# A contraction-outer first pair, and new places in SBUF, in a transformer layer with split fp32 matmuls

## Chip, cores and metric

One NeuronCore of one Trainium2 chip runs the whole kernel in one launch. The metric is the device time in microseconds. Three runs of the kernel before gave 1034.02, 1034.82 and 1034.90; the median is 1034.82.

## What is computed

One layer of a streaming encoder on 512 tokens of width 1024, all in float32. The reference, cut to what matters:

```python
x = x + 0.5 * swiglu(rms_norm(x, ffn1_norm), ffn1_gate, ffn1_up, ffn1_down)
x = x + hybrid_mixer(rms_norm(x, mix_norm), w_in, ...)      # GLA | diff attention | short conv, then w_out
x = x + 0.5 * swiglu(rms_norm(x, ffn2_norm), ffn2_gate, ffn2_up, ffn2_down)
return rms_norm(x, final_norm)

def swiglu(h, w_gate, w_up, w_down):                        # w_gate, w_up: 1024 x 2816, w_down: 2816 x 1024
    return (jax.nn.silu(h @ w_gate) * (h @ w_up)) @ w_down
```

## The kernel before

Activations stand transposed: features on the 128 partitions, the 512 tokens in the free dimension. x is KT = 8 tiles of 128x512. TensorE works in a float32 format (fp32r) that holds less than float32, so both operands of each large product are split into a high and a low part, and each 128x128x512 block takes three matmuls (`three`, L379 to L383): hi by hi, hi by lo, lo by hi, summed in one PSUM bank.

The operands are made on the chip. ACT makes xg_hi = gain * x (`operand_hi`, L776) and DVE makes xg_lo = gain * x - xg_hi (`operand_lo`, L1061). Weights arrive from HBM in slabs of 128x1024 (up, 8 k-tiles) or 128x1408 (down, 11 k-tiles of the inner 22) in `raw`, a buffer of two slots; slab s lies in slot s % 2. ACT copies a slab to w_hi (`split_hi`, L766), DVE subtracts to get w_lo (`split_lo`, L1052). SP loads slab s when slab s-2 has been split (`lo_ready`), ACT splits it when the product of slab s-2 is through (`slab_used`). Slabs are counted through the kernel: 44 up slabs of FFN 1 (gate and up in turn), 16 down slabs, the mixer's, 8 of w_out, 44, 16.

The division by the root mean square comes after the product, as a factor per token: squares of x are summed over the tiles in sq_sum, TensorE sums them over the partitions (`mean_squares`, L398), ACT takes the root, DVE inverts it into a diagonal (`invert`, L1077), TensorE spreads that over the partitions (`spread_rms`, L406), ACT copies it to rinv. DVE then multiplies the PSUM results of gate and up by rinv (L1109, L1113), ACT applies silu, DVE multiplies the two, and the result is split into h_hi and h_lo, the moving operands of the down products. The mixer leaves its result in mixed_hi and mixed_lo, the moving operands of w_out. Three projections of the mixer are made the other way round, in natural layout: there xg is the stationary operand and w_hi and w_lo move, 384 columns at a time.

At the start SP issues, in this order, the load of slab 0, the eight x tiles, slab 1 and seven small constants. ACT issues the gain's DMA and loads its table for the root. ACT's order of work is then xg_hi of tile 0, split of slab 0, xg_hi of tiles 1 to 7, split of slab 1, the squares of x tiles 4 to 7; DVE's is the low parts in the same order. GpSimd squares x tiles 0 to 3 and adds all eight into sq_sum. TensorE runs WARM_UP = 14 small matmuls on ones, then the product of slab 0 (waiting for each xg_lo in turn), of slab 1, the mean squares, slab 2, the spread, slab 3, and the start products (a table of the attention's bias, and lambda), and from there in loops a pair of slabs for each of the 22 tiles of the inner width.

Every engine's order is written out by hand, and the waits are on counting semaphores. SBUF places follow from the order of the `sb(...)` declarations: each tensor lies behind the one declared before, and what is declared in an inner `with` block is given back at its end, so that the next declarations take the same place. Two lines set the first products:

```python
pe.wait_ge(xg_lo_ready, first_use + k + 1)                  # L418, before each k-tile of the first product
last = product(g + 1, 2 + b, None, n)                       # L440, the up product, after the gate product
```

## Times and profile before

| | |
|---|---|
| median of 3 runs | 1034.82 us (1034.02 to 1034.90) |
| profiled execution: its own time / its span | 1036.32 us / 1034.5 us |
| granted TensorE clock, mean over the span | 0.987 |
| busy: TensorE / DVE / ACT / GpSimd | 98% / 49% / 34% / 9% |
| HBM traffic | 94 MB, 91 GB/s over the span |

Busy shares are averages over the whole span. A TensorE that is busy is not at its peak, since matmuls overlap: what one costs in a dense stretch is read from the distance between the starts of consecutive ones and not from their durations. The profiled execution took 1.5 us more than the median of the runs.

### The profile page before, as it was taken

The page shows a single profiled execution, that of the slowest core. Times are in us where ns is not written, and L with a number is a line of the kernel's source. Part 1 is how long each engine was busy: PE and PEld are TensorE (multiplying, and loading weights), DVE is VectorE, ACT ScalarE, POOL GpSimd, SP SyncE. Part 2 cuts the span into 40 slices and gives each one's busy share as a digit, 9 for nine tenths or more (in the row PEclk, how much of TensorE's full clock was granted, in tenths as well). Part 3 has the DMA queues.
Part 4 walks back from the last instruction along what each step waited for, and adds up shares of the span by engine and source line. Part 5 has one row for each costly group of instructions (what it writes and reads, how often), then busy time and mean ns, then how long its engine had stood idle before and what let it go on. Part 6 is the DMA issues. An engine that isn't in the chain of part 4 may idle for free.

```text
span 1034.5 us, 13356 instructions
## 1 busy us (share of the span) xinstructions
PE 1010.6 (98%) x5044; PEld 832.2 (80%) x5044; DVE 504.9 (49%) x719; ACT 353.8 (34%) x475; POOL 90.2 (9%) x87
## 2 busy tenths in 40 slices
PE   7999999999999999999989999999999999999996
PEld 4888888888888888777878788788888888888886
DVE  7444444444334433767556864444444444423223
ACT  4443434443221222444723233332332232322221
POOL 6000000000012224000012004300000000000002
PEclk8999999999999999999989999999999999999998
DMA  5233223233322225212211113223222222322312
GB/s 177 90 102 100 85 99 101 83 103 113 111 85 95 101 61 163 72 62 67 71 37 62 54 69 102 82 102 101 84 99 101 101 86 96 131 85 88 108 56 82
DMA packets 27457, 94.89 MB, mean 92 GB/s; under 512 B 3760, under 2 KB 5968, under 8 KB 27424
## 3 DMA queue, kind: packets, MB, share of 16 engines
q1 hardware_dynamic: 26384, 92.03, 26.6%
q0 software_dynamic: 896, 2.39, 0.8%
q8 instruction: 22, 0.36, 0.1%
q14 instruction: 11, 0.09, 0.0%
q10 hardware_dynamic: 144, 0.02, 0.0%
HBM read 92.00 MB, written 2.42 MB: 91 GB/s over the span
## 4 chain that ended last, share of the span: by engine, by line
PE 45%; DVE 3%; ACT 1%; issue 1%; POOL 0%; DVEq 0%; POOLq 0%
PE ps L381 14%; PE ps L382 14%; PE ps L383 14%; PE ps L609 1%; DVE x L1190 1%; DVE e_dec L1287 1%; DVE a_comp L1307 0%; ACT w_hi L774 0%; PE ps L641 0%; PE ps L649 0%; PE ps L579 0%; DVE w_lo L1058 0%; DVE states L1333 0%; PE ps L485 0%; DVE e_dec L1314 0%
## 5 line engine op out<-in xcount | busy, mean ns | idle before, releaser
L381 PE MATMUL ps<-xg_hi,w_hi 128*128 128x512 f32 x848 | 336.5, 397 | 7.5 <-DVE w_lo L1058 3.4
L382 PE MATMUL ps<-xg_lo,w_hi 128*128 128x512 f32 x848 | 331.7, 391 | 0.0
L383 PE MATMUL ps<-xg_hi,w_lo 128*128 128x512 f32 x848 | 331.5, 391 | 0.0
L774 ACT ACTIVATE w_hi<-raw 128x1024 fp32r<-128x1024 f32 (+2 forms) x155 | 174.6, 1127 | 456.3 <-PE ps L383 455.3
L1058 DVE TENSOR_TENSOR w_lo<-raw,w_hi 128x1024 fp32r<-128x1024 f32 (+2 forms) x155 | 208.2, 1343 | 191.3 <-ACT w_hi L774 191.2
L381 PEld LDWEIGHTS ps<-xg_hi,w_hi 128*128 128x128 f32 x848 | 160.0, 189 | 52.5 <-issue 8.7
L383 PEld LDWEIGHTS ps<-xg_hi,w_lo 128*128 128x128 f32 x848 | 160.2, 189 | 34.0
L382 PEld LDWEIGHTS ps<-xg_lo,w_hi 128*128 128x128 f32 x848 | 160.3, 189 | 31.8
L381 PE MATMUL ps<-h_hi,w_hi 128*128 128x512 f32 (+1 forms) x374 | 142.9, 382 | 0.0
L383 PE MATMUL ps<-h_hi,w_lo 128*128 128x512 f32 (+1 forms) x374 | 142.7, 382 | 0.0
L382 PE MATMUL ps<-h_lo,w_hi 128*128 128x512 f32 (+1 forms) x374 | 142.7, 382 | 0.0
L1113 DVE TENSOR_TENSOR up_s<-ps,rinv 128x512 f32<-128x512 f32 x44 | 30.4, 691 | 112.7 <-PE ps L383 112.7
L382 PEld LDWEIGHTS ps<-h_lo,w_hi 128*128 128x128 f32 x374 | 70.2, 188 | 15.1
L381 PEld LDWEIGHTS ps<-h_hi,w_hi 128*128 128x128 f32 x374 | 70.2, 188 | 15.1
L383 PEld LDWEIGHTS ps<-h_hi,w_lo 128*128 128x128 f32 x374 | 70.2, 188 | 15.0
L842 ACT ACTIVATE h_hi<-up_s 128x512 f32 (+1 forms) x44 | 27.8, 632 | 85.4 <-DVE up_s L1118 85.4
L1135 DVE SCALAR_TENSOR_TENSOR x<-ps,x 128x512 f32 (+1 forms) x23 | 15.8, 688 | 70.9 <-PE ps L383 70.9
L1109 DVE TENSOR_TENSOR gate_s<-ps,rinv 128x512 f32<-128x512 f32 x44 | 30.4, 691 | 41.0 <-PE ps L383 36.4
L1120 DVE TENSOR_TENSOR h_lo<-up_s,h_hi 128x512 f32 (+1 forms) x44 | 30.4, 692 | 38.8 <-ACT h_hi L842 38.8
L1064 DVE SCALAR_TENSOR_TENSOR xg_lo<-x,gain,xg_hi 128x512 fp32r<-128x512 f32 (+1 forms) x24 | 32.5, 1373 | 13.3 <-ACT xg_hi L778 13.3
L371 POOL TENSOR_TENSOR x<-x,rinv 128x256 f32<-128x256 f32 x6 | 5.4, 926 | 363.2 <-ACT rinv L802 363.2
L381 PE MATMUL ps<-w_hi,xg_hi 128*128 128x384 f32 x96 | 33.2, 346 | 0.0
(171 smaller groups left out, 816.8 us busy)
## 6 DMA issues: line engine op xcount, KB each, us to landing
raw<-up_w SPq DMA_DIRECT2D x88, 512.0 KB, 3.2
raw<-down_w SPq DMA_DIRECT2D x32, 704.0 KB, 4.0
raw<-t_w SPq DMA_DIRECT2D x18, 512.0 KB, 3.3
raw<-out_w SPq DMA_DIRECT2D x8, 512.0 KB, 3.3
raw<-nat_w SPq DMA_DIRECT2D x6, 576.0 KB, 3.9
x<-xT SPq DMA_DIRECT2D x8, 256.0 KB, 5.2
out<-x SPq DMA_DIRECT2D x8, 256.0 KB, 2.3
raw<-nat_w SPq DMA_DIRECT2D x3, 384.0 KB, 3.2
```

Source lines behind the costliest of these rows:

```text
L381: pe.matmul(out_ap, a[0], b[0], start=first, stop=False)
L382: pe.matmul(out_ap, a[0], b[1], start=False, stop=False)
L383: return pe.matmul(out_ap, a[1], b[0], start=False, stop=last)
L609: last = pe.matmul(ps[c * CHUNK:(c + 1) * CHUNK, bank + hd, col + b * CHUNK:col + (b + 1) * CHUNK], a, bb, start=True, stop=True)
L774: act.activation(w_hi[:, slot(s), 0:w], raw[:, slot(s), 0:w], ACT.Copy).then_inc(hi_ready, 1)
L842: act.activation(h_hi[:, m, :], up_s[:, b, :], ACT.Copy).then_inc(h_hi_ready, 1)
L1058: dve.tensor_tensor(w_lo[:, slot(s), 0:w], raw[:, slot(s), 0:w], w_hi[:, slot(s), 0:w], ALU.subtract).then_inc(lo_ready, 1)
L1064: dve.scalar_tensor_tensor(xg_lo[:, k, :], x[:, k, :], gain[:, gi, bass.ds(k, 1)], xg_hi[:, k, :], ALU.mult, ALU.subtract).then_inc(xg_lo_ ...
L1109: dve.tensor_tensor(gate_s[:, b, :], ps[:, b, :], rinv[:], ALU.mult).then_inc(gate_scaled, 1)
L1113: dve.tensor_tensor(up_s[:, b, :], ps[:, 2 + b, :], rinv[:], ALU.mult).then_inc(up_scaled, 1)
L1120: dve.tensor_tensor(h_lo[:, m, :], up_s[:, b, :], h_hi[:, m, :], ALU.subtract)\
L1135: dve.scalar_tensor_tensor(x[:, k, :], ps[:, bank, :], scale, x[:, k, :], ALU.mult, ALU.add)\
```

## The change

It has two parts.

**The first pair.** Slabs 0 and 1 (gate and up of the first inner tile) are no longer two products one after the other. `first_pair` runs over the eight k-tiles on the outside, and inside over the two slabs: six matmuls per k-tile, into banks 0 and 2. The two slabs come in PIECES = 4 pieces of 256 columns (two k-tiles), by eight DMAs on ACT's queue; slab 0 has buffers of its own (first_raw, first_hi, first_lo), slab 1 has slot 1, and slab 2 finds slot 0 free. ACT and DVE split the pieces between the operand tiles. The squares of x are now all ACT's, in eight buffers, and their sum is DVE's; GpSimd has none at the start. The mean squares come after slab 2 (before: after slab 1), the spread in the middle of slab 3 (before: after slab 2). WARM_UP is 24.

**The places.** x, raw, rinv, sq_sum, ones, ident and the small constants are declared last. xg, w_hi and w_lo come first, then h or mixed. In KB per partition, counted from the first of the kernel's tensors, by the declared sizes:

| | before | after |
|---|---|---|
| xg_hi, xg_lo | 16 to 48 | 0 to 32 |
| w_hi, w_lo | 59 to 81 | 32 to 54 |
| h_hi | 87.6 to 131.6 | 54 to 98 |
| h_lo | 131.6 to 175.6 | 98 to 142 |
| mixed_hi, mixed_lo | 87.6 to 119.6 | 54 to 86 |
| x | 0 to 16 | 173.1 to 189.1 |
| raw | 48 to 59 | 189.1 to 200.1 |

The diff, cut to its core:

```diff
-WARM_UP = 14
+WARM_UP = 24
+PIECES = 4
+PIECEW = UPW // PIECES
...
-        x = sb("x", [P, KT, S])
         xg_hi = sb("xg_hi", [P, KT, S], F32R)
         xg_lo = sb("xg_lo", [P, KT, S], F32R)
-        raw = sb("raw", [P, 2, SLOTW])
         w_hi = sb("w_hi", [P, 2, SLOTW], F32R)
         w_lo = sb("w_lo", [P, 2, SLOTW], F32R)
-        rinv = sb("rinv", [P, S])
-        sq_sum = sb("sq_sum", [P, S])
-        ones = sb("ones", [P, P])
...
             sq = sb("sq", [P, S], stack=st)
+            first_raw = sb("first_raw", [P, UPW], stack=st)
+            first_hi = sb("first_hi", [P, UPW], F32R, stack=st)
+            first_lo = sb("first_lo", [P, UPW], F32R, stack=st)
...
-        onehot_s = pT[0:32].rearrange("b a s -> b (a s)")[:, 0:5 * P]
+        onehot_s = dv[0:32].rearrange("b a f -> b (a f)")[:, 5 * P:10 * P]
...
+        sb("end_of_stages", [P, 64])
+        x = sb("x", [P, KT, S])
+        raw = sb("raw", [P, 2, SLOTW])
+        rinv = sb("rinv", [P, S])
...
-            load(0, up_w[0, 0, 0])
             for k in range(KT):
                 sp.dma_start(x[:, k, :], xT[k]).then_inc(x_loaded[k], 16)
-            load(1, up_w[0, 0, 1])
+            load(2, up_w[0, 1, 0])
...
+            load(3, up_w[0, 1, 1])
...
+            def first_pair():
+
+                for k in range(KT):
+                    q, rest = divmod(k, KT // PIECES)
+                    if rest == 0:
+                        if q < PIECES - 1:
+                            pe.wait_ge(piece_lo, 2 * (q + 1))
+                        else:
+                            wait_slab(1)
+                    pe.wait_ge(xg_lo_ready, k + 1)
+                    for s, (_, hi, lo) in enumerate(first_slabs):
+                        kk = slice(k * P, (k + 1) * P)
+                        last = three(ps[:, 2 * s, :], (hi[:, kk], lo[:, kk]), (xg_hi[:, k, :], xg_lo[:, k, :]),
+                                     k == 0, k == KT - 1)
+                        if k == KT - 1:
+                            last.then_inc(slab_used, 1)
...
-                    if isinstance(i, int) and m == 1 and phase == 0:
-                        spread_rms(phase)
-                    if first and phase:
+                    second = isinstance(i, int) and m == 1 and phase == 0
+                    if second or (first and phase):
                         mean_squares(phase)
-                    last = product(g + 1, 2 + b, None, n)
+                    last = product(g + 1, 2 + b, None, n, spread_at=KT // 2 if second else None)
...
             act.dma_start(gain[:], gains).then_inc(gain_loaded, 16)
+            for q in range(PIECES):
+                for s, (first, _, _) in enumerate(first_slabs):
+                    act.dma_start(first[:, piece(q)], up_w[0, 0, s][:, piece(q)]).then_inc(piece_loaded[q], 16)
...
-            for k in range(KT - 4, KT):
-                act.activation(start_sq[k - (KT - 4)], x[:, k, :], ACT.Square).then_inc(start_squared, 1)
+            split_hi(2)
+            for k in range(KT):
+                if k == KT - 1:
+                    act.wait_ge(lo_ready, 1)
+                act.activation(start_sq[k], x[:, k, :], ACT.Square).then_inc(start_squared if k else sq_added, 1)
...
+            split_lo(2)
+            for k in range(1, KT):
+                dve.wait_ge(start_squared, k)
+                dve.wait_ge(sq_added, k)
+                dve.tensor_tensor(sq_sum[:], sq_sum[:], start_sq[k], ALU.add).then_inc(sq_added, 1)
```

How the order of the instructions moves, at three places. (L numbers of the change are those of its own file.) First ACT at the start, up to its third operand tile, before and now:

```order
L764 DMA gain<-gains 128x32
L806 ACT_TABLE_LOAD
L806 ACTIVATE root_scrap<-eps_t 128x1 [waits consts_set]
L778 ACTIVATE xg_hi<-x,gain 128x512 [waits x_loaded0,gain_loaded]
L774 ACTIVATE w_hi<-raw 128x1024 [waits raw_loaded0]
L778 ACTIVATE xg_hi<-x,gain 128x512 [waits x_loaded1]
L778 ACTIVATE xg_hi<-x,gain 128x512 [waits x_loaded2]
```

```order
L793 DMA first_raw<-up_w 128x256
L793 DMA raw<-up_w 128x256
L835 ACT_TABLE_LOAD
L835 ACTIVATE root_scrap<-eps_t 128x1 [waits consts_set]
L807 ACTIVATE xg_hi<-x,gain 128x512 [waits x_loaded0,gain_loaded]
L929 ACTIVATE first_hi<-first_raw 128x256 [waits piece_loaded0]
L929 ACTIVATE w_hi<-raw 128x256
L807 ACTIVATE xg_hi<-x,gain 128x512 [waits x_loaded1]
L807 ACTIVATE xg_hi<-x,gain 128x512 [waits x_loaded2]
```

The first two rows of the second piece are the last of the eight new DMAs, which stand between the gain's DMA and the table load. The hi parts come in quarters.

Second DVE, from slab 1's low half (before) or slab 2's (now) to the diagonal:

```order
L1058 TENSOR_TENSOR w_lo<-raw,w_hi 128x1024 [waits hi_ready]
L1199 TENSOR_TENSOR lamprod<-lamin 48x2 [waits start_loaded]
L1058 TENSOR_TENSOR w_lo<-raw,w_hi 128x1024 [waits hi_ready] x2
L1080 RECIPROCAL rnat<-rnat 128x4 [waits rms_ready]
L1082 TENSOR_SCALAR rinv<-ident,rnat 128x128 [waits dve_result]
```

```order
L1094 TENSOR_TENSOR w_lo<-raw,w_hi 128x1024 [waits hi_ready]
L1245 TENSOR_TENSOR sq_sum<-sq_sum,gate_s 128x512 [waits sq_added,start_squared] x2
L1245 TENSOR_TENSOR sq_sum<-sq_sum,up_s 128x512 [waits sq_added,start_squared] x2
L1245 TENSOR_TENSOR sq_sum<-sq_sum,sq 128x512 [waits sq_added,start_squared]
L1245 TENSOR_TENSOR sq_sum<-sq_sum,rinv 128x512 [waits sq_added,start_squared]
L1245 TENSOR_TENSOR sq_sum<-sq_sum,first_raw 128x512 [waits sq_added,start_squared]
L1247 TENSOR_TENSOR lamprod<-lamin 48x2 [waits start_loaded]
L1094 TENSOR_TENSOR w_lo<-raw,w_hi 128x1024 [waits hi_ready]
L1116 RECIPROCAL rnat<-rnat 128x4 [waits rms_ready]
L1118 TENSOR_SCALAR rinv<-ident,rnat 128x128 [waits dve_result]
```

Seven adds have come to DVE, between the low halves of slabs 2 and 3.

Third TensorE, the last k-tile of the first pair now and the first matmul of slab 2:

```order
L386 MATMUL ps<-xg_hi,first_hi 128x512 [waits xg_lo_ready]
L387 MATMUL ps<-xg_lo,first_hi 128x512
L388 MATMUL ps<-xg_hi,first_lo 128x512
L386 MATMUL ps<-xg_hi,w_hi 128x512
L387 MATMUL ps<-xg_lo,w_hi 128x512
L388 MATMUL ps<-xg_hi,w_lo 128x512
L386 MATMUL ps<-xg_hi,w_hi 128x512 [waits lo_ready]
```

A wait for xg_lo stands before each group of six matmuls, where it stood before each group of three.

## Rows read from the trace of the kernel before

**Rows 1.** The page: busy us (share of the span) and instructions of each engine

```profile
PE 1010.6 (98%) x5044; PEld 832.2 (80%) x5044; DVE 504.9 (49%) x719; ACT 353.8 (34%) x475; POOL 90.2 (9%) x87
```

**Rows 2.** Timeline, TensorE, 0 to 44 us: start, us, instruction, idle before

```profile
1.01 5.32 PE L519 MATMUL ps<-ones 128*128 128x128 f32 x28 [1.01 <-POOL one_t L333]
8.46 0.80 PE L381 MATMUL ps<-xg_hi,w_hi 128*128 128x512 f32 x1 [2.13 <-DVE w_lo L1058]
...
22.02 0.71 PE L381 MATMUL ps<-xg_hi,w_hi 128*128 128x512 f32 x1 [1.26 <-DVE w_lo L1058]
...
29.19 0.95 PE L402 MATMUL ps<-ones,sq_sum 128*128 128x1 f32 x8
30.00 0.49 PE L381 MATMUL ps<-xg_hi,w_hi 128*128 128x512 f32 x1
...
35.58 1.05 PE L410 MATMUL ps<-rinv,ones 128*128 128x128 f32 x8
...
42.02 1.34 PE L392 MATMUL ps<-pT,relb 32*128 32x512 f32 x4
...
43.60 0.50 PE L381 MATMUL ps<-xg_hi,w_hi 128*128 128x512 f32 x1
```

**Rows 3.** Stretches, TensorE: us, busy (instructions), granted clock, DMA share, GB/s

```profile
12.00:19.00 7.00, 4.49 (x15) 1.00 0.16 59
...
22.00:26.00 4.00, 3.98 (x10) 0.57 0.58 168
```

**Rows 4.** Timeline, DVE, 8 to 43 us

```profile
8.32 11.42 DVE L1064 SCALAR_TENSOR_TENSOR xg_lo<-x,gain,xg_hi 128x512 fp32r<-128x512 f32 x7
...
41.84 1.22 DVE L1058 TENSOR_TENSOR w_lo<-raw,w_hi 128x1024 fp32r<-128x1024 f32 x1
```

**Rows 5.** Line L1064, xg_lo: shortest, median and longest duration in ns

```profile
L1064 DVE SCALAR_TENSOR_TENSOR xg_lo<-x,gain,xg_hi x24: 740/1644/1785, 5.6 to 660.3; 128x512 fp32r<-128x512 f32 x16, - x8
```

**Rows 6.** Timeline, TensorE, an up product: two starts 24 matmuls apart

```profile
200.36 0.39 PE L382 MATMUL ps<-xg_lo,w_hi 128*128 128x512 f32 x1
...
205.80 0.39 PE L382 MATMUL ps<-xg_lo,w_hi 128*128 128x512 f32 x1
```

**Rows 7.** Timeline, TensorE, down products: two starts 66 matmuls apart

```profile
300.06 0.40 PE L382 MATMUL ps<-h_lo,w_hi 128*128 128x512 f32 x1
...
315.46 0.40 PE L382 MATMUL ps<-h_lo,w_hi 128*128 128x512 f32 x1
```

**Rows 8.** Timeline, TensorE, natural layout: two starts 27 matmuls apart

```profile
385.75 0.33 PE L382 MATMUL ps<-w_lo,xg_hi 128*128 128x384 f32 x1
...
390.43 0.33 PE L382 MATMUL ps<-w_lo,xg_hi 128*128 128x384 f32 x1
```

**Rows 9.** Groups by form, TensorE: count, busy us, mean ns of one

```profile
L382 PE MATMUL ps<-xg_lo,w_hi 128*128 128x512 f32 x848 | 331.7, 391 | 0.0
...
L382 PE MATMUL ps<-h_lo,w_hi 128*128 128x512 f32 x330 | 130.3, 395 | 0.0
...
L382 PE MATMUL ps<-mixed_lo,w_hi 128*128 128x512 f32 x64 | 25.3, 395 | 0.0
```

**Rows 10.** Timeline, ACT and its queue, 0 to 14 us

```profile
0.75 0.41 ACTq L764 DMA_DIRECT2D gain<-gains  x1
1.19 1.28 ACT L806 ACT_TABLE_LOAD   x1 [1.19 <-PEq L1570]
2.48 0.20 ACT L806 ACTIVATE root_scrap<-eps_t 128x1 f32<-128x1 f32 x1
4.86 0.72 ACT L778 ACTIVATE xg_hi<-x,gain 128x512 fp32r<-128x512 f32 x1 [2.17 <-DMA x<-xT]
...
12.06 1.06 ACT L774 ACTIVATE w_hi<-raw 128x1024 fp32r<-128x1024 f32 x1 [0.88 <-DMA raw<-up_w]
13.02 1.14 ACT L899 ACTIVATE gate_s<-x 128x512 f32<-128x512 f32 x2
```

**Rows 11.** Timeline, SP's queue: the issue of the x tiles

```profile
1.20 3.90 SPq L279 DMA_DIRECT2D x<-xT  x8
```

More of the change, by code:

```diff
@@ L100, with piece @@
 LAST_MEAN, LAST_SPREAD = 4, 12
+def piece(q):
+    return slice(q * PIECEW, (q + 1) * PIECEW)
 def half_tokens(c):
@@ L188, in build_layer @@
         shared = sb("shared", [P, 4, S])
+        sb("end_of_stages", [P, 64])
+        x = sb("x", [P, KT, S])
+        raw = sb("raw", [P, 2, SLOTW])
+        rinv = sb("rinv", [P, S])
+        sq_sum = sb("sq_sum", [P, S])
+        ones = sb("ones", [P, P])
+        ident = sb("ident", [P, P])
+        gain = sb("gain", [P, 4, KT])
+        eps_t = sb("eps_t", [P, 1])
+        one_t = sb("one_t", [P, 1])
+        root_scrap = sb("root_scrap", [P, 1])
+        rnat = sb("rnat", [P, NB])
+        lam = sb("lam", [P, 4])
+        convw = sb("convw", [P, 2, 3])
+        gla_g = sb("gla_g", [P, DV])
+        diff_g = sb("diff_g", [P, DV])
+        relb = sb("relb", [32, P])
+        lamin = sb("lamin", [DK, 4])
+        lamprod = sb("lamprod", [DK, 2])
         a_full = e_dec
@@ L202, in build_layer @@
         STAT = 7
-        start_sq = [t[:, b, :] for t in (gate_s, up_s) for b in range(2)]
+        start_sq = [sq_sum[:], *(t[:, b, :] for t in (gate_s, up_s) for b in range(2)), sq[:], rinv[:],
+                    first_raw[:, 0:S]]
+        first_slabs = [(first_raw[:], first_hi[:], first_lo[:]), (raw[:, 1, :], w_hi[:, 1, :], w_lo[:, 1, :])]
         x_loaded = [sem(f"x_loaded{k}") for k in range(KT)]
@@ L212, in build_layer @@
         raw_loaded = [sem("raw_loaded0"), sem("raw_loaded1")]
+        piece_loaded = [sem(f"piece_loaded{q}") for q in range(PIECES)]
+        piece_hi, piece_lo = sem("piece_hi"), sem("piece_lo")
         out_stored = sem("out_stored")
@@ L262, in load @@
             def load(s, src, n=0):
-                if not (isinstance(n, int) and s + n < 2):
+                if not (isinstance(n, int) and s + n < 3):
                     sp.wait_ge(lo_ready, n + (s - 1))
@@ L268, in load_ffn @@
             def load_ffn(f, up0, dn0):
-                first = 1 if up0 == 0 else 0
+                first = 2 if up0 == 0 else 0
                 with sp.Fori(first, FT) as m:
@@ L769, in split_hi @@
                     return
-                if not (isinstance(n, int) and s + n < 2):
+                if not (isinstance(n, int) and s + n < 3):
                     act.wait_ge(slab_used, n + (s - 1))
@@ L827, in next_hi @@
                             split_hi(s + c, n)
-                    next_hi(2)
+                    if not (first and f == 0):
+                        next_hi(2)
                     if first:
@@ L892, in _ @@
             for k in range(KT):
+                q, rest = divmod(k, KT // PIECES)
                 act.wait_ge(x_loaded[k], 16)
                 operand_hi(0, k, 0)
-                if k == 0:
-                    split_hi(0)
-            split_hi(1)
-            for k in range(KT - 4, KT):
-                act.activation(start_sq[k - (KT - 4)], x[:, k, :], ACT.Square).then_inc(start_squared, 1)
+                if rest == 0:
+                    act.wait_ge(piece_loaded[q], 32)
+                    for first, hi, _ in first_slabs:
+                        act.activation(hi[:, piece(q)], first[:, piece(q)], ACT.Copy)\
+                            .then_inc(piece_hi if q < PIECES - 1 else hi_ready, 1)
+            split_hi(2)
[3 more added lines that the diff above has]
+                act.activation(start_sq[k], x[:, k, :], ACT.Square).then_inc(start_squared if k else sq_added, 1)
             ffn_up(0, UP1)
@@ L1100, in pair @@
                     if first:
-                        next_lo(2)
                         if f == 0:
                             next_lo(3)
+                        else:
+                            next_lo(2)
                         invert(2 * f)
@@ L1193, in _ @@
             for k in range(KT):
+                q, rest = divmod(k, KT // PIECES)
                 operand_lo(0, k, 0)
-                if k == 0:
-                    split_lo(0)
-            split_lo(1)
+                if rest == 0:
+                    for s, (first, hi, lo) in enumerate(first_slabs):
+                        if q < PIECES - 1:
+                            dve.wait_ge(piece_hi, 2 * q + s + 1)
+                        else:
+                            dve.wait_ge(hi_ready, s + 1)
+                        dve.tensor_tensor(lo[:, piece(q)], first[:, piece(q)], hi[:, piece(q)], ALU.subtract)\
+                            .then_inc(piece_lo if q < PIECES - 1 else lo_ready, 1)
+            split_lo(2)
[3 more added lines that the diff above has]
+                dve.tensor_tensor(sq_sum[:], sq_sum[:], start_sq[k], ALU.add).then_inc(sq_added, 1)
             dve.wait_ge(start_loaded, 16 * 7)
```

39 lines of the change are left out of this document (11 added, 28 removed).

## The prediction

> **What bounds the kernel now.** I read the page first: TensorE is busy 98% of the span [rows 1], so whatever another engine saves counts only where TensorE waits for it, and what a matmul costs counts everywhere. I then looked for what the 2% is, in the starts of TensorE's groups [rows 2]: 28 warm-up records from 1.01, the first product from 8.46, the second from 22.02, the mean squares at 29.19. A product is 8 k-tiles of three matmuls, 24 in all. The first took 13.6 us, and between 12 and 19 us TensorE was busy 4.49 of 7 us at the full clock [rows 3]: it waits there for xg_lo. DVE made seven xg_lo from 8.32 in 11.42 us, 1.6 us each [rows 4], where the same instruction takes 0.74 at best [rows 5]; GpSimd squares x beside it. The second product ran from 22 to 26 us at a granted share of 0.57 [rows 3], mostly the 1.2 GHz level, after that thin stretch.
>
> Then I looked at what a matmul costs with TensorE never waiting, as the distance of two starts. Moving operand xg: 24 matmuls from 200.36 to 205.80, 0.2267 us each [rows 6]. Moving operand h: 66 from 300.06 to 315.46, 0.2333 each [rows 7]. Natural-layout matmuls, which move w_hi and w_lo, 384 columns: 27 from 385.75 to 390.43, 0.1733 each [rows 8]. Against 512 and 384 columns at 2.4 GHz (0.2133 and 0.1600) the surplus is 13.3 ns for xg and w and 20 ns for h. The grouped rows say the same for mixed: 395 ns as for h, against 391 for xg [rows 9]. What these have in common is the place. Counted in KB per partition from the kernel's first tensor, xg lies at 16 to 48, w_hi and w_lo at 59 to 81, mixed at 87.6 to 119.6, h_hi and h_lo at 87.6 to 175.6. So the cheap ones lie below 81 and the dear ones above 87.6.
>
> **The start, step by step.** Removed: GpSimd's squares, so I take xg_lo at 0.75. Added on ACT's queue: eight piece DMAs behind the gain's, ahead of its table load. ACT's own DMA took 0.41 [rows 10], SP's eight x DMAs took 3.90 from first to last, 0.49 each [rows 11]. I take 0.47: the ninth ends at about 4.9. The table load (1.28) and the scrap root (0.20) follow [rows 10], so the first xg_hi starts at 6.4, where it was 4.86. That is a loss of 1.5 us; the x tile itself will have been there. xg_hi 0.72, two hi pieces of 256 columns at some 0.35 each (between nothing and a half of the 1.06 that 1024 columns took, near a third since 512 take 0.57 in the pair of squares at 13.02) [rows 10]; on DVE xg_lo 0.75 and two lo pieces at some 0.4 (1024 take 1.22 [rows 4]). The first step is complete at 6.4+0.7+0.75, with DVE's two pieces behind: 8.7. The warm-up has 48 records instead of 28. At the spacing of the first ones, 5.32 us for 28 [rows 2], it would end at 10; the later ones ran at the high level, so I take 8.2 to 9.7 and start the first pair at 8.7.
>
> From there, per two k-tiles, ACT needs about 2.1 us, DVE 2.2, and the transfers 768 KB: the 3 MB of the start had landed by 12.06, when ACT's wait for slab 1 ended [rows 10], so some 2.2 us. TensorE needs 12 x 0.2267 = 2.7. So TensorE sets the pace and runs dense: 48 x 0.2267 = 10.9, ending at 19.7. Before, the same 48 matmuls ended at 29.19. That is 9.5 us gained at this point, 1.5 lost on ACT included.
>
> What is late next? Slab 2 (slot 0 is free from the beginning) is split by about 16.8: no wait. Its product ends at 25.3. The squares, eight on ACT at 0.57 from 15.6 and seven adds on DVE, end at 21: the mean squares at 25.3 do not wait. They cost 0.81 (29.19 to 30.00) [rows 2]. Slab 3 starts at 26.1; its split waited for slot 1 (19.7) and is done by 22.5. The spread of the root now stands at its middle, at 28.9; the root and DVE's diagonal need under 2 us from 26.0, so it does not wait. Slab 3 ends at 32.5, the start products (42.02 to 43.60, 1.6 us) [rows 2] at 34.2. **Now a wait appears.** Slab 4's low half stands on DVE behind rinv, gate, up, silu, h of tile 0 and gate of tile 1. Before, that chain led from the spread at 35.58 [rows 2] to w_lo at 41.84, ready at 43.06 [rows 4]: 7.5 us, covered by a whole product and the start products. The chain is unchanged, so it ends at 28.9 + 7.5 = 36.4, and TensorE, free at 34.2, waits 2.2 us. Slab 4 starts at 36.4 instead of 43.60: **7.2 us gained**. Everything behind it is the old order. Bounds: 8.5 if the chain is shorter by a microsecond; 4 if the ACT queue issues at half that rate (3.8 later, mostly handed on), or if the new wait puts the clock down again (the slow stretch of 22 to 26 cost 1.7).
>
> **The homes.** Over the whole kernel 3 x 330 full-width matmuls move h and 3 x 64 move mixed [rows 9]. In the new layout xg is at 0 to 32 KB, w at 32 to 54, mixed_hi at 54 to 70, mixed_lo at 70 to 86, h_hi at 54 to 98, h_lo at 98 to 142. I assume that a moving operand below the border has the cheap surplus, 6.67 ns less, and that the border is between 81.0 and 87.6 KB; by the middle, h_hi's tiles 0 to 14 get cheap, and all but one of mixed. That is 2 x 15 in each of 15 output tiles = 450, and 184 of mixed: 634 x 6.67 ns = **4.2 us**. Between 81.0 and 87.6 it is 3.7 to 4.5. If the cause is nearness of some other kind (the groups differ also in alignment: xg and w start at multiples of 512 bytes from the first tensor, h and mixed 128 bytes beyond one, and now all of them at multiples), all 1182 get cheap: 7.9 us. Lower end: zero, or a loss if the lowest place is not cheap (below). The half-width last tile (132 matmuls) I leave out; at most 0.9. x, raw and the constants at the top: ACT and DVE read them beside TensorE's work, and DVE is busy 49% [rows 1]; at nothing, and if every one of them took 5% longer the slabs would still be split one product ahead.
> The Trainium skill speaks against this term: "TensorE: Matmul & The Clock Gate", Back-to-back issue gap, gives the distance of two matmuls by the columns and the clock alone, about 216 ns for 512, no address in it, and "SBUF — State Buffer", Who interferes with whom, says PE never waits on anyone. By it the homes would be worth nothing. The trace does not agree: it has two distances for the same shape.
>
> **Sum.** The profiled execution: 1036.32, with a span of 1034.5, 1.5 above the median of the runs shown (1034.82), to which I apply the difference: 1034.8 - 7.2 - 4.2 = **1023.4**. 0.2% is 2.1 us, about what a measurement of this kernel can tell from no change.
>
> **Rivals.**
> A (forecast), 0.38: start 7.2, part of h and mixed cheap: 1023.4, own range 1021 to 1026.
> B, 0.25: it is not the height, and all of h and mixed get cheap: 1034.8 - 7.2 - 7.9 = 1019.7. For it: h shows one distance over 88 KB, with no grading by height.
> C, 0.15: the homes change nothing, and the two distances belong to the stages: 1027.6. For it: after a stall xg too runs some ten matmuls near 0.233. Against: mixed and h share the distance in unlike stages.
> D, 0.08: the start gives only 4 (the ACT queue, or the clock), homes as in A: 1026.6.
> E, 0.09: a further step down: xg and w, now lower than anything in the trace, drop as well. 3 x 848 matmuls move xg [rows 9]; at another 6.67 ns that is 17 us: about 1006.
> F, slower, 0.05: the cheap places are a band between 16 and 81 KB and not the bottom. Then xg, moved to 0 to 32, pays 6.67 ns on the matmuls that move it from below 16 (xg_hi, two in three: 1696) or on all 2544: 11.3 or 17.0 us. It decides from 11.4 on, what A gains: 1023.4 + 11.3 = 1034.7 or 1040.4.
>
> **How the numbers follow.** The predicted time is A's. The range holds A, B, C and D, reaching 3 us past B for a start that gives more and 2 past C: 1016.5 to 1029.5; E and F are outside. Faster by over 0.2%: A to E, 0.95 less 0.02 for a start that fails in more ways than D: 0.93. Within 0.2%: part of F and that remainder, 0.03. Slower: 0.04.
>
> **What would show it.** In the profile after: the first product matmul at 8 to 10 us, 48 of them without a wait and the mean squares near 25; GpSimd with no squares there; xg_lo near 0.75; a wait of about 2 us before slab 4, on w_lo, at 34 to 36; DVE's w_lo for it ready 7.5 after the spread. For the homes: the distance of two h matmuls, 0.2333 before; A wants about 0.2302 in the mean of an output tile, cheap in the first tiles of h_hi and dear in h_lo, B 0.2267 throughout, C 0.2333. xg at 0.2267 would refute E and F. Wrong would be a wait between k-tiles of the first pair (a piece late by DMA), a granted clock of 0.5 inside it, or a product further on that waits for a split.

## The result

The changed kernel took 1024.58 us (median of 4 runs, 1023.38 to 1024.96), beside 1034.42 (4 runs, 1033.99 to 1034.90) of the kernel before. The ratio of the two is 0.9896, with a 95% interval of 0.9884 to 0.9908: 1.0% faster, and 9.8 us by the medians. 1023.4 had been forecast. The profiled execution took 1024.96, with a span of 1023.0: 11.5 us less than the span of before.

The busy line of the page after, which answers to [rows 1], and the granted clock in 40 slices:

```profile
PE 1002.9 (98%) x5064; PEld 835.2 (82%) x5064; DVE 500.9 (49%) x732; ACT 356.3 (35%) x485; POOL 73.4 (7%) x76
...
PEclk9899999999999999999989999999999999999998
```

TensorE is still the bound. GpSimd has lost the 17 us of its squares.

TensorE's timeline after, 0 to 44 us, which answers to [rows 2] (start, us, instruction, idle before and its releaser):

```profile
1.00 7.51 PE L545 MATMUL ps<-ones 128*128 128x128 f32 x48 [1.00 <-POOL one_t L346]
9.34 0.50 PE L386 MATMUL ps<-xg_hi,first_hi 128*128 128x512 f32 x1 [0.83 <-DVE w_lo L1239]
...
20.12 0.39 PE L388 MATMUL ps<-xg_hi,w_lo 128*128 128x512 f32 x1
20.35 0.39 PE L386 MATMUL ps<-xg_hi,w_hi 128*128 128x512 f32 x1
...
25.80 0.95 PE L407 MATMUL ps<-ones,sq_sum 128*128 128x1 f32 x8
26.61 0.47 PE L386 MATMUL ps<-xg_hi,w_hi 128*128 128x512 f32 x1
...
29.46 1.06 PE L415 MATMUL ps<-rinv,ones 128*128 128x128 f32 x8
...
34.47 0.38 PE L401 MATMUL ps<-lamprod,ones 48*128 48x2 f32 x2
37.00 0.79 PE L386 MATMUL ps<-xg_hi,w_hi 128*128 128x512 f32 x1 [2.15 <-DVE w_lo L1094]
37.59 0.63 PE L387 MATMUL ps<-xg_lo,w_hi 128*128 128x512 f32 x1
...
41.86 0.63 PE L388 MATMUL ps<-xg_hi,w_lo 128*128 128x512 f32 x1
```

The first pair runs from 9.34 to 20.35 with no wait between its k-tiles. The mean squares stand at 25.80 (before: 29.19), the spread at 29.46 (35.58). Then comes the forecast wait for slab 4's low half; its first matmul starts at 37.00, where it was 43.60: 6.6 us earlier. Behind the wait the matmuls stand 0.427 us apart instead of 0.227 (37.59 to 41.86: 10 distances in 4.27 us). Twelve do, and the thirteenth in part. From slab 4's first matmul to the first down product they make 220.31 us, where the kernel before took 217.73: 2.6 us are lost again. The stretches of this part, which answer to [rows 3], show the granted clock there: of the stretch from 36 to 44 us a large part is at the 1.2 GHz level.

```profile
34.00:44.00 10.00, 7.85 (x24) 0.66 0.38 131
36.00:44.00 8.00, 7.00 (x19) 0.59 0.47 164
...
12.00:19.00 7.00, 7.00 (x33) 1.00 0.50 152
```

(Columns as there: us, TensorE busy and its instructions, granted clock, DMA share, GB/s.) From 12 to 19 us TensorE is now busy all the time, 4.49 of 7 us before.

ACT and its queue after, up to the second piece, which answers to [rows 10]:

```profile
0.75 0.41 ACTq L790 DMA_DIRECT2D gain<-gains  x1
1.20 0.46 ACTq L793 DMA_DIRECT2D first_raw<-up_w  x1
...
3.62 0.64 ACTq L793 DMA_DIRECT2D raw<-up_w  x1
4.29 0.69 ACTq L793 DMA_DIRECT2D first_raw<-up_w  x1
5.01 0.68 ACTq L793 DMA_DIRECT2D raw<-up_w  x1
5.72 1.28 ACT L835 ACT_TABLE_LOAD   x1 [5.72 <-issue]
7.01 0.20 ACT L835 ACTIVATE root_scrap<-eps_t 128x1 f32<-128x1 f32 x1
7.12 0.71 ACT L807 ACTIVATE xg_hi<-x,gain 128x512 fp32r<-128x512 f32 x1
```

The nine DMAs hold ACT to 5.7 us and not to 4.9: the last three took 0.64 to 0.69 each, the earlier ones 0.41 to 0.46. SP's eight x tiles, which answer to [rows 11], were issued from 0.76 in 4.05 us.

DVE after, which answers to [rows 4], and under it line L1100, the answer to [rows 5] (shortest, median, longest in ns):

```profile
9.21 1.40 DVE L1100 SCALAR_TENSOR_TENSOR xg_lo<-x,gain,xg_hi 128x512 fp32r<-128x512 f32 x2
...
35.73 1.22 DVE L1094 TENSOR_TENSOR w_lo<-raw,w_hi 128x1024 fp32r<-128x1024 f32 x1
```

```profile
L1100 DVE SCALAR_TENSOR_TENSOR xg_lo<-x,gain,xg_hi x24: 739/753/1781, 7.9 to 651.8; 128x512 fp32r<-128x512 f32 x16, - x8
```

xg_lo takes 0.75 at the start; the median over the kernel fell from 1644 ns to 753. Slab 4's low half stands at 35.73 and is ready at 36.95.

What a matmul costs in the dense stretches after, as in [rows 6] and [rows 7]: xg, two starts 24 matmuls apart, and h, two starts 66 apart:

```profile
195.66 0.39 PE L387 MATMUL ps<-xg_lo,w_hi 128*128 128x512 f32 x1
...
201.10 0.39 PE L387 MATMUL ps<-xg_lo,w_hi 128*128 128x512 f32 x1
...
290.18 0.39 PE L387 MATMUL ps<-h_lo,w_hi 128*128 128x512 f32 x1
...
305.14 0.39 PE L387 MATMUL ps<-h_lo,w_hi 128*128 128x512 f32 x1
```

That is 5.44/24 = 0.2267 for xg, as before, and 14.96/66 = 0.2267 for h, 0.2333 before. Mixed stands at 0.2267 too. The natural layout [rows 8] has 27 matmuls from 377.16 to 381.87, 0.1744 each, for 0.1733. By form, the answer to [rows 9], xg_lo still takes 391 ns, and h_lo and mixed_lo take 389, for 395 before.

The starts of the stages on TensorE show where the 11.5 us of span came from:

| first matmul of | before | after | earlier by | gained in the stage |
|---|---|---|---|---|
| down product of FFN 1 | 261.3 | 257.3 | 4.0 | the start: 4.0 (6.6 less 2.6) |
| natural layout | 384.5 | 377.0 | 7.5 | 3.5 |
| w_out | 611.6 | 604.4 | 7.2 | -0.4 |
| FFN 2 | 656.3 | 647.9 | 8.4 | 1.3 |
| down product of FFN 2 | 898.4 | 889.9 | 8.4 | 0.0 |
| the last matmul of it | 1023.1 | 1011.7 | 11.4 | 2.9 |

The stages in which h or mixed moves gained 3.5 + 1.3 + 2.9 = 7.7 us; 1182 matmuls by 6.67 ns are 7.9. The mixer's 0.4 is within what this stage varies by: from the natural layout to w_out the kernels below took 225.9 to 228.5 us, and the kernel before took 227.0.

The 6.6 us at slab 4 hold something that is not the change's. In the profiled execution of the kernel before, the second product ran at half clock from 22 to 26 us [rows 3]. Two kernels below have the same old start and differ from it in places alone (the new places with the old start, and the padded kernel before). In their profiled executions the granted clock from 22 to 26 us is 1.00, and slab 4 starts at 42.04 and 42.10 and not at 43.60. So 1.5 us of the 11.5 belong to one execution, and against those two the new start brings slab 4 forward by 5.1 us.

### The profile page after: what moved, and what is told of

It reads as the page before. It is cut to its first block, busy times and chain, and to the rows that moved or that the text cites. A ratio compares the mean times of both kernels' runs of the same rounds, so it can differ in the third digit from the quotient of the medians.

```text
span 1023.0 us, 13402 instructions
## 1 busy us (share of the span) xinstructions
PE 1002.9 (98%) x5064; PEld 835.2 (82%) x5064; DVE 500.9 (49%) x732; ACT 356.3 (35%) x485; POOL 73.4 (7%) x76
## 4 chain that ended last, share of the span: by engine, by line
PE 45%; DVE 3%; ACT 1%; issue 1%; POOL 0%; DVEq 0%; POOLq 0%
PE ps L386 14%; PE ps L387 14%; PE ps L388 14%; DVE x L1227 1%; PE ps L635 1%; DVE e_dec L1335 1%; DVE a_comp L1355 1%; ACT w_hi L803 0%; PE ps L667 0%; PE ps L675 0%; PE ps L605 0%; DVE w_lo L1094 0%; DVE states L1381 0%; PE ps L511 0%; DVE e_dec L1362 0%
## 5 line engine op out<-in xcount | busy, mean ns | idle before, releaser
L386 PE MATMUL ps<-xg_hi,w_hi 128*128 128x512 f32 x840 | 332.2, 395 | 3.0 <-DVE w_lo L1094 2.1
L1094 DVE TENSOR_TENSOR w_lo<-raw,w_hi 128x1024 fp32r<-128x1024 f32 (+2 forms) x153 | 204.0, 1334 | 181.1 <-ACT w_hi L803 181.0
L1100 DVE SCALAR_TENSOR_TENSOR xg_lo<-x,gain,xg_hi 128x512 fp32r<-128x512 f32 (+1 forms) x24 | 26.0, 1092 | 15.7 <-ACT xg_hi L807 15.7
L387 PE MATMUL ps<-w_lo,xg_hi 128*128 128x384 f32 x96 | 32.7, 341 | 0.0
```

The costliest lines, as they stand in the source:

```text
L386: pe.matmul(out_ap, a[0], b[0], start=first, stop=False)
L387: pe.matmul(out_ap, a[0], b[1], start=False, stop=False)
L1094: dve.tensor_tensor(w_lo[:, slot(s), 0:w], raw[:, slot(s), 0:w], w_hi[:, slot(s), 0:w], ALU.subtract).then_inc(lo_ready, 1)
L1100: dve.scalar_tensor_tensor(xg_lo[:, k, :], x[:, k, :], gain[:, gi, bass.ds(k, 1)], xg_hi[:, k, :], ALU.mult, ALU.subtract).then_inc(xg_lo_ ...
```

## The experiments

None of these kernels leaves out a part of the layer. Where no wait and no order is named, only places in SBUF differ.

**The two parts alone.** First the new start with the old places, and then the new places with the old start.

```diff
+        x = sb("x", [P, KT, S])
         xg_hi = sb("xg_hi", [P, KT, S], F32R)
         xg_lo = sb("xg_lo", [P, KT, S], F32R)
+        raw = sb("raw", [P, 2, SLOTW])
...
-        sb("end_of_stages", [P, 64])
-        x = sb("x", [P, KT, S])
-        raw = sb("raw", [P, 2, SLOTW])
...
```

> The new start with the old places (x first, h at 87.6 KB). My account of the change: the start alone gives what the two traces show at slab 4, 6.6 us earlier, less 2.6 for the half-clock stretch behind the new wait: 4.0 us, so about 1030.4, and h and mixed matmuls stay 0.2333 us apart. Rival (the start gives the whole forecast 7.2 and the clock stretch is an accident of one execution): 1027. Rival (the start needs the new places): no gain.

Measured: 1031.84 us, beside 1035.12 of the kernel before, a ratio of 0.9962 (0.9947 to 0.9977). h stayed at 0.2333. Slab 4 stood at 37.37:

```profile
34.83 0.38 PE L400 MATMUL ps<-lamprod,ones 48*128 48x2 f32 x2
37.37 0.50 PE L385 MATMUL ps<-xg_hi,w_hi 128*128 128x512 f32 x1 [2.16 <-DVE w_lo L1093]
37.71 0.40 PE L386 MATMUL ps<-xg_lo,w_hi 128*128 128x512 f32 x1
37.95 0.39 PE L387 MATMUL ps<-xg_hi,w_lo 128*128 128x512 f32 x1
```

The wait is that of the changed kernel, and yet this execution shows no half clock behind it: its matmuls stand 0.23 apart at once, and its granted clock from 34 to 44 us is 1.00. Up to the first down product (at 255.1) the start was worth 6.2 us here, 1.5 of them the half clock of the kernel before's own execution, and about 4 us in the runs. Those fall into two groups: 1028.96 and 1029.31 (the profiled one), and 1031.84 to 1032.58. The distance is that of the half clock behind the wait, but the slower ones have no profile, so that this is their cause is not shown.

```diff
-        x = sb("x", [P, KT, S])
         xg_hi = sb("xg_hi", [P, KT, S], F32R)
         xg_lo = sb("xg_lo", [P, KT, S], F32R)
-        raw = sb("raw", [P, 2, SLOTW])
...
+        sb("end_of_stages", [P, 64])
+        x = sb("x", [P, KT, S])
+        raw = sb("raw", [P, 2, SLOTW])
...
```

> The old start with the new places. My account: all 1182 matmuls that move h or mixed get 6.67 ns cheaper, 7.9 us, less some tenths in the mixer: 1026.5 to 1027. Height theory of the prediction (only what lies below 87.6 KB): 1030.2, with h_lo matmuls dear; it is already in trouble, since h_lo at 98 to 142 KB is cheap in the changed kernel.

Measured: 1027.76 us, ratio 0.9929 (0.9912 to 0.9946). h and mixed both at 0.2267 throughout, h_lo at 98 to 142 KB included. 0.71% of 1034.8 is 7.3 us, by the interval 5.6 to 9.1: all 1182 matmuls would give 7.9, and the 634 only 4.2. The two parts give 0.38% and 0.71%, together 1.09%, and the change gave 1.04%: they add up.

**Height or alignment.** The kernel before, with a gap of 384 bytes ahead of h and mixed. They lie higher than before by it, and at a multiple of 512 bytes.

```diff
+        sb("ahead_of_h", [P, 96])
         with ExitStack() as st:
             h_hi = sb("h_hi", [P, FT, S], F32R, stack=st)
```

> The kernel before with 384 unused bytes ahead of h and mixed, nothing else: they lie at 88 KB and above, but now at multiples of 512 bytes from xg, w_hi and w_lo. Alignment theory: h and mixed matmuls 0.2267 us apart, 7.9 us faster: 1026.5. Height theory: 0.2333 as before, 1034.4. Theory of neighbours (x and raw, written and read by others, must be away from the operands): 1034.4 as well.

```profile
290.66 0.39 PE L382 MATMUL ps<-h_lo,w_hi 128*128 128x512 f32 x1
...
305.62 0.39 PE L382 MATMUL ps<-h_lo,w_hi 128*128 128x512 f32 x1
```

14.96/66 = 0.2267 at 88 KB and above, with x, raw and the constants where they had been. The time was 1028.23, ratio 0.9935 (0.9919 to 0.9952), that of the new places (1027.76). One line of padding gives what the whole move of the tensors gives.

The opposite: the changed kernel, with a gap of 128 bytes ahead of h and mixed.

```diff
+        sb("ahead_of_h", [P, 32])
         with ExitStack() as st:
             h_hi = sb("h_hi", [P, FT, S], F32R, stack=st)
```

> The changed kernel with 128 unused bytes ahead of h and mixed: they stand 128 bytes beyond a multiple of 512 from w_hi, as in the kernel before, but low. Alignment theory: h and mixed matmuls 0.2333 us apart, 7.9 us slower than the changed kernel: 1032.5. Height or neighbours: 0.2267, 1024.6.

```profile
290.17 0.39 PE L387 MATMUL ps<-h_lo,w_hi 128*128 128x512 f32 x1
...
305.57 0.39 PE L387 MATMUL ps<-h_lo,w_hi 128*128 128x512 f32 x1
```

15.40/66 = 0.2333 at 54 KB: low down and dear. 1031.67 us, 7.1 more than the changed kernel, and a ratio of 0.9973 (0.9940 to 1.0006) to the kernel before.

**An operand's own place, or its place against the other operand's.** All operands moved by 128 bytes together, and then w_hi and w_lo alone.

```diff
+        sb("ahead_of_all", [P, 32])
         xg_hi = sb("xg_hi", [P, KT, S], F32R)
```

> The changed kernel with 128 unused bytes ahead of everything: all operands moved by 128 bytes together. If the place relative to the other operand (the stationary w, loaded meanwhile) decides: 0.2267 everywhere, 1024.6. If the absolute place decides: 0.2333 everywhere, for xg too, 3700 matmuls by 6.67 ns = 25 us slower, 1049.

Measured: 1022.82 us (2 runs), ratio 0.9872 (0.9827 to 0.9916), span 1019.5. xg, h and mixed are all at 0.2267, though every operand lies 128 bytes off its place in the changed kernel. Its profiled execution had the wait before slab 4 (idle for 2.15 us) and no half clock behind it; its stretch from 34 to 44 us, beside the 0.66 of the changed kernel:

```profile
34.00:44.00 10.00, 7.85 (x36) 1.00 0.41 134
```

So 2.6 of the 3.5 us between the two spans are the clock.

```diff
+        sb("ahead_of_w", [P, 32])
         w_hi = sb("w_hi", [P, 2, SLOTW], F32R)
         w_lo = sb("w_lo", [P, 2, SLOTW], F32R)
+        sb("behind_w", [P, 96])
```

> The changed kernel with w_hi and w_lo alone moved by 128 bytes, xg and h left. If the relation between the moving and the stationary operand decides: xg, h and mixed all stand 384 bytes beyond, none as w, and all matmuls lose 6.67 ns: 25 us slower, about 1049, the natural-layout ones too. If only the moving operand's own place decides: xg, h and mixed stay 0.2267 and only the natural-layout ones, which move w, get dearer: 1024.6 plus 1 to 2.

```profile
195.31 0.39 PE L389 MATMUL ps<-xg_lo,w_hi 128*128 128x512 f32 x1
...
200.91 0.39 PE L389 MATMUL ps<-xg_lo,w_hi 128*128 128x512 f32 x1
```

5.60/24 = 0.2333 for xg, and the same for h and mixed in FFN 1 and w_out: 1044.39 us (one run), 9.4 us slower than the kernel before beside it (1034.97) and 19.8 slower than the changed kernel. xg stood where it stands in the changed kernel, h and mixed 512 bytes further. w's own place can't be the cause, since it was moved just as far in the run before and nothing got dearer. **What decides is the moving operand's start against the stationary operand's.** The 25 us of the expectation did not come whole. In FFN 2 xg stands 0.2325 apart (24 distances from 700.14 to 705.72) at the same offset, and the natural layout, where w moves against xg, got dearer by 2 ns and not by 6.7: its first 27 distances are 0.1763 each (386.17 to 390.93), for 0.1744 in the changed kernel.

**Which offsets.** First a scan: tiles of h 2080 bytes apart instead of 2048, so that the offset grows by 32 bytes from one k-tile to the next.

```diff
-            h_hi = sb("h_hi", [P, FT, S], F32R, stack=st)
-            h_lo = sb("h_lo", [P, FT, S], F32R, stack=st)
+            h_hi = sb("h_hi", [P, FT, S + 8], F32R, stack=st)
+            h_lo = sb("h_lo", [P, FT, S + 8], F32R, stack=st)
...
```

> The changed kernel with a stride of 2080 bytes instead of 2048 between the 22 tiles of h_hi and of h_lo, so that tile k starts 32k bytes beyond a multiple of 512: one down product scans the offsets 0 to 672. Alignment theory: the distance of two matmuls depends on k, 0.2267 at offset 0 and again at 512 (k = 16), 0.2333 at 128 (k = 4) and at 640 (k = 20); what lies between tells the granule. Theory without alignment: 0.2267 for all k.

Measured: 1028.91 us (one run); h at 0.2323 in the mean (290.54 to 305.87, 66 matmuls). The three matmuls of one k-tile took 683 to 710 ns in the mean of seven output tiles, with a pattern that came back after eight k-tiles (8 by 32 = 256 bytes) in the second half of the product, but also at offset 0 never the 680 of the aligned kernel. With offsets that change from one k-tile to the next an offset does not fix the distance, perhaps because the neighbouring matmul counts too. So they can't be read off here: inconclusive by itself, and what follows is for offsets that stay the same. Hence two kernels with a constant offset for each operand. In the first the starts of xg, h and mixed lie 256, 64 and 32 bytes off w's (modulo 512), in the second 64, 256 and 384.

```diff
+        sb("ahead_of_w", [P, 64])
...
+            sb("ahead_of_h", [P, 16], stack=st)
...
+        sb("ahead_of_mixed", [P, 8])
```

> The changed kernel with other offsets of the moving operand against w_hi and w_lo, in bytes modulo 512: xg 256, h 64, mixed 32. Granule 512 (only offset 0 is cheap): all at 0.2333, some 25 us slower than the changed kernel, about 1049. Granule 256: xg stays 0.2267, h and mixed 0.2333, about 1032.5. Granule 64: xg and h cheap, mixed 0.2333, about 1026. What 128 and 384 cost is known: 0.2333.

h at an offset of 64 bytes and mixed at 32, two starts 66 and 24 matmuls apart:

```profile
290.23 0.39 PE L390 MATMUL ps<-h_lo,w_hi 128*128 128x512 f32 x1
...
305.34 0.39 PE L390 MATMUL ps<-h_lo,w_hi 128*128 128x512 f32 x1
...
604.02 0.39 PE L390 MATMUL ps<-mixed_lo,w_hi 128*128 128x512 f32 x1
...
609.62 0.40 PE L390 MATMUL ps<-mixed_lo,w_hi 128*128 128x512 f32 x1
```

15.11/66 = 0.2289 and 5.60/24 = 0.2333; xg at 256 bytes: 195.37 to 200.81, 0.2267. The time was 1026.58 (one run), near the 1026 of granule 64, but by the distances none of the three granules fits: 64 bytes cost 2.2 ns, a third of what 128 cost.

```diff
+        sb("ahead_of_w", [P, 112])
...
+            sb("ahead_of_h", [P, 64], stack=st)
...
+        sb("ahead_of_mixed", [P, 96])
```

> As the run before, with xg at 64, h at 256, mixed at 384. Granule 512: all at 0.2333, about 1049. Granule 256: h stays 0.2267, xg and mixed 0.2333, about 1043. Granule 64: xg and h cheap, mixed 0.2333, about 1026. If what decides is tied to the operand and not to its offset, xg and h trade no places between the two runs.

Measured: 1031.67 us (one run). xg at 64 bytes: 195.51 to 201.01, 24 apart, 0.229; h at 256 bytes: 290.00 to 304.96, 0.2267; mixed at 384: 608.21 to 613.79, 0.2325. All of it in one table:

| offset between the starts, bytes | ns from one matmul to the next | seen in |
|---|---|---|
| 0 | 226.7 | xg, h, mixed of the changed kernel; all three moved together |
| 256 | 226.7 | xg in the one, h in the other of the last two |
| 64 | 228.9 to 229.2 | h in the one, xg in the other |
| 32 | 233.3 | mixed in the first of the last two |
| 128 | 233.3 | h and mixed before; the changed kernel with h moved |
| 384 | 232.5 to 233.3 | the changed kernel with w moved; mixed in the last |

So far as these offsets tell, what counts is the offset modulo 256 bytes: 0 and 256 agree, and 128 and 384 within 1 ns. xg and h trade places between the last two runs, so it is not tied to the operand.

**The new wait.** The changed kernel, with slab 4's split brought forward: ACT's part right behind the root, DVE's right behind `invert`.

```diff
-                    if not (first and f == 0):
+                    if f or not (isinstance(i, int) and m < 2):
                         next_hi(2)
...
                         root(2 * f)
-                        if f:
-                            next_hi(3)
+                        next_hi(3 if f else 4)
...
                         invert(2 * f)
-                        if f:
-                            next_lo(3)
+                        next_lo(3 if f else 4)
```

> The changed kernel with the split of slab 4 taken ahead: ACT does the high half right behind the root, DVE the low half right behind the diagonal. Theory (the new wait ahead of slab 4 is order alone, and the half-clock stretch comes from it): TensorE goes through from slab 3 to slab 4, no half clock there, 2.4 + 2.6 us gained on the changed kernel: 1019.6. Rival (the wait moves to slab 5 or to the PSUM banks, which gate and up of the first tiles free later): 1022 to 1024. Rival (the half clock has another cause): 1022.

Measured: 1019.59 us (4 runs, 1018.75 to 1020.05), ratio 0.9845 (0.9828 to 0.9861). DVE, then TensorE, then the stretch from 34 to 44 us:

```profile
28.13 1.22 DVE L1093 TENSOR_TENSOR w_lo<-raw,w_hi 128x1024 fp32r<-128x1024 f32 x1
```

```profile
34.51 0.38 PE L401 MATMUL ps<-lamprod,ones 48*128 48x2 f32 x2
34.82 0.50 PE L386 MATMUL ps<-xg_hi,w_hi 128*128 128x512 f32 x1
35.16 0.39 PE L387 MATMUL ps<-xg_lo,w_hi 128*128 128x512 f32 x1
```

```profile
34.00:44.00 10.00, 10.00 (x45) 1.00 0.22 76
```

Slab 4 follows the start products without a wait, and the clock stays up. Against the changed kernel that is 5.0 us in the medians and 4.9 in the spans: 2.2 of the wait and, in the profiled executions, 2.6 of the slow matmuls that in the changed kernel stood behind it (from slab 4 to the down product 217.74 us, for 220.31).

**ACT's nine DMAs.** The kernel just shown, with six of the eight pieces issued by SP between the x tiles and the warm-up shortened.

```diff
-WARM_UP = 24
+WARM_UP = 16
...
                 sp.dma_start(x[:, k, :], xT[k]).then_inc(x_loaded[k], 16)
+                if k % 2 and k < KT - 1:
+                    q = (k + 1) // 2
+                    for s, (first, _, _) in enumerate(first_slabs):
+                        sp.dma_start(first[:, piece(q)], up_w[0, 0, s][:, piece(q)]).then_inc(piece_loaded[q], 16)
...
-            for q in range(PIECES):
+            for q in range(1):
```

> The kernel with slab 4's split ahead, and ACT now issues only the gain and the two first pieces; the other six go out on SP's queue between the x tiles. WARM_UP is 16, since the first pair can begin earlier. Theory (ACT's eight DMA issues ahead of its table load set the start of the first pair): ACT's first xg_hi at about 4.2 instead of 7.1 us, the first pair from 6.5 instead of 9.4, and 2.8 us less: 1016.8. Rival (the transfers are the limit: the last piece had landed only at 14.7): k-tile 6 waits for its pieces, and 1 us or nothing is left: 1018.6 to 1019.6.

```profile
3.83 0.72 ACT L811 ACTIVATE xg_hi<-x,gain 128x512 fp32r<-128x512 f32 x1 [0.17 <-DMA gain<-gains]
6.04 0.42 ACT L932 ACTIVATE first_hi<-first_raw 128x256 fp32r<-128x256 f32 x1 [1.49 <-DMA raw<-up_w]
```

xg_hi starts 3.3 us earlier than in the changed kernel, but then ACT waits 1.49 us for the first piece: the issue is no longer late, the landing is. The first pair starts at 7.55, where 6.5 had been expected, and runs to 18.56 without a wait, so the rival's late k-tile did not come either. Slab 4 stands at 32.99, 1.8 us ahead of the kernel above. Measured: 1018.07 us (1017.25 to 1021.93), ratio 0.9846 (0.9824 to 0.9867). The median is 1.5 us lower and the ratio against the kernel before the same, so whether the runs gained anything by it is open.

**What of the start did it.** The kernel before with its old order of products and its old places. Only the squares left GpSimd (ACT squares, DVE adds, slab 2's split in their middle), and the mean squares and the spread moved to the places of the change. WARM_UP stays at 14.

```diff
-            for k in range(KT):
-                if k < KT - 4:
-                    pool.wait_ge(x_loaded[k], 16)
-                    square_tile(0, k)
...
+            for k in range(KT):
+                if k == KT // 2:
+                    split_hi(2)
+                act.activation(start_sq[k], x[:, k, :], ACT.Square).then_inc(start_squared if k else sq_added, 1)
...
+            for k in range(1, KT):
+                if k == KT // 2:
+                    split_lo(2)
...
+                dve.tensor_tensor(sq_sum[:], sq_sum[:], start_sq[k], ALU.add).then_inc(sq_added, 1)
```

> The kernel before with one part of the new start: GpSimd has no squares, ACT makes all eight and DVE adds them (with the split of slab 2 in their middle), mean squares and spread stand where the change puts them. The two first products stay one after the other, slabs in one DMA each, old places, WARM_UP 14. Theory A (what held TensorE was DVE's xg_lo at 1.6 us beside GpSimd, and the order of the first pair matters little): xg_lo takes 0.75, the second product ends near 20 to 21 us instead of 29, as in the changed kernel, slab 4 begins near 37, and the time is that of the new start alone, 1031 to 1032. Theory B (the outer contraction carries the gain, since in the old order every xg_lo feeds three matmuls only): the second product ends at 25 or later, and at most 2 us are gained: 1033.

DVE's seven xg_lo, and TensorE's first products, mean squares and slab 4:

```profile
7.75 4.72 DVE L1060 SCALAR_TENSOR_TENSOR xg_lo<-x,gain,xg_hi 128x512 fp32r<-128x512 f32 x7
```

```profile
7.88 0.50 PE L373 MATMUL ps<-xg_hi,w_hi 128*128 128x512 f32 x1 [1.99 <-DVE w_lo L1054]
14.63 0.50 PE L373 MATMUL ps<-xg_hi,w_hi 128*128 128x512 f32 x1 [0.96 <-DVE w_lo L1054]
25.64 0.94 PE L394 MATMUL ps<-ones,sq_sum 128*128 128x1 f32 x8
...
36.84 0.50 PE L373 MATMUL ps<-xg_hi,w_hi 128*128 128x512 f32 x1 [2.16 <-DVE w_lo L1054]
```

Seven xg_lo in 4.72 us instead of 11.42 [rows 4], 0.67 each: the second product starts at 14.63, and not at 22.02 [rows 2]. The mean squares stand at 25.64 (25.80 in the changed kernel), slab 4 at 36.84 (37.00). Measured: 1031.83 us, ratio 0.9963 (0.9949 to 0.9977), the same as the whole new start with old places (1031.84, 0.9962). **The start's gain is that of the squares' move off GpSimd, with the new places of the mean squares and the spread;** these two were not tried apart. The contraction-outer order with its pieces added nothing that these runs can tell: it runs dense, but starts 1.5 us later (9.34 for 7.88), since the pieces' DMAs stand on ACT's queue.

## Why the prediction was right, and where its steps were not

That the time came out at the forecast is luck in part: two steps erred in opposite directions. By the profiled spans 7.2 + 4.2 = 11.4 us had been forecast and 11.5 came: 4.0 at the start and 7.5 from the places. By the medians only 9.8 came, since the base of the sum was off as well.

- **First pair, removed wait for xg_lo**: right. 8.7 to 19.7 had been forecast, 9.34 to 20.35 came, with no wait inside and xg_lo at 0.75. The 0.6 us are ACT's queue: xg_hi at 6.4 had been forecast and came at 7.12, since I took 0.47 for every DMA and the last three took 0.64 to 0.69. The Trainium skill, "SBUF — State Buffer", Who interferes with whom, says that a DVE instruction with two SBUF inputs contends with a GpSimd instruction that reads SBUF. The trace agrees: 1.6 us each with GpSimd's squares beside them, 0.75 or less without.
- **The base of the sum**: wrong by 1.5 us, and no bound of the prediction covers it. It measured the start's gain against slab 4 at 43.60, in an execution with a half-clock stretch from 22 to 26 us, and took it off the median. The same old start reached slab 4 at 42.04 and 42.10 in two other executions, without that stretch. This is about what separates the 11.5 us of the spans from the 9.8 of the medians.
- **"So TensorE sets the pace"**: true of the trace, but it credited the wrong part. It held the new order to be what makes the first 48 matmuls dense. With the squares moved alone they are nearly as dense, and start earlier.
- **"Now a wait appears"**: right. 2.2 us before slab 4 had been forecast; from the last start product to slab 4 there are 2.53 us (34.47 to 37.00), and 0.31 in the kernel without the wait (34.51 to 34.82), so the wait is 2.2; and the chain from the spread to w_lo ready was 7.5 (29.46 to 36.95) as forecast. Slab 4 at 36.4 had been forecast and was at 37.00. DVE's work ahead of it came later than forecast, slab 2's low half at 18.2 for 16.8, the last square at 23.6 for 21 and slab 3's low half at 24.8 for 22.5, all still in time.
- **The clock behind that wait**: the mis-sized term. It stood among the bounds at 1.7 us and not in the sum; it cost 2.6. With the 0.6 above, that makes the start 4.0 instead of 7.2. It does not come every time. Nine of the profiled executions have this wait: two ran some thirteen matmuls at the 1.2 GHz level behind it (2.6 us in the changed kernel), four ran seven or eight (about 1.5 us), and three none (listed at the end). The sum should have carried a part of it.
- **The homes, "I assume that a moving operand below the border has the cheap surplus"**: this step failed. There is no border of height. h at 88 KB and above is cheap with 384 bytes ahead of it, and at 54 KB it is dear with 128. What had been rival B (all 1182 matmuls cheap, 7.9 us) is what happened, and the stages gave 7.7. The argument that stood for B, that h shows one distance over 88 KB with no grading, should have weighed more: a border just between two groups of tensors is a coincidence, while the tensors' offsets (0 and 128 bytes) could be worked out from the declarations. B's own wording, multiples of 512 bytes, was not right either: it is the offset between the two operands, modulo 256.
- **C, E and F** fell: the places alone gave 0.71%, and xg stayed at 0.2267. **D**'s price for the start, 4 us, came true beside homes that gave more.
- **The rule set against the homes** was that of the Trainium skill, "TensorE: Matmul & The Clock Gate", Back-to-back issue gap: a distance by columns and clock, with no address in it. Its 216 ns for 512 columns are there the gap of an isolated matmul, and for a sustained stream the section has about 131. The runs show neither, but 226.7, 228.9 and 233.3 for the same shape at the same clock, by the offset. That PE never waits on anyone ("SBUF — State Buffer", Who interferes with whom) they do not contradict: the padded kernel before kept all its neighbours and was as fast as the moved one.
- The half-width matmuls, left out "at most 0.9", went the other way, by 1.3 ns each (below).

Open: why the offset counts (no experiment reached into the mechanism), and what decides whether the clock falls behind a wait of 2.2 us.

## What to carry to other kernels

Work out from the declarations where the moving and the stationary operand of the dense matmuls start: in this kernel an offset that is a multiple of 256 bytes saved 6.7 ns of 233, and one line of padding did it. Before reordering a product whose operands come late, look at what runs beside the engine that makes them: taking GpSimd's squares away, with the mean squares and the spread moved to fit, gave the whole gain of the start. Look at a second profile before an execution is taken for the kernel: here 1.5 us of the old start were the clock of one execution. And when a change makes TensorE earlier, follow the next operand's chain and bring its split forward with it: the wait of 2.2 us and the slow matmuls behind it were worth 5.0 us, and the version without them, at 1019.59, beats both kernels by a clear interval (a ratio of 0.9828 to 0.9861, for 0.9884 to 0.9908 of the changed kernel).
